# Hybrid decoder trunk on one core: the 16-block inverse multiplied from the left, and T transposed once

## What is computed

```python
    def step(state, inp):
        r_t, w_t, k_t, v_t, kk_t, b_t = inp
        sa = jnp.einsum('bhvk,bhk->bhv', state, kk_t)
        state = (state * w_t[:, :, None, :] - sa[..., None] * b_t[:, :, None, :]
                 + v_t[..., None] * k_t[:, :, None, :])
        return state, jnp.einsum('bhvk,bhk->bhv', state, r_t)
```

## Time and profile before

| | |
|---|---|
| three runs: median, lowest, highest | 1014.09, 1011.42, 1014.51 us |
| the profiled execution: its time | 1012.7 us |
| its span, from the first to the last instruction | 1010.9 us |
| TensorE busy | 973.7 us, 96% of the span |
| mean granted clock of TensorE, as a share of 2.4 GHz | 0.981 |
| VectorE, ScalarE, GpSimd busy | 262.8, 173.8, 74.5 us |
| rounds of the inverse in layer 0, in layer 1 (from the span's start) | 117.4 to 156.6, 537.5 to 576.3 us |

### The profile page before, as it was taken

One profiled execution on the slowest core, in us unless ns is written; L12 is line 12 of the kernel. 1 busy time (PEld: TensorE's weight loads), 2 busy tenths in 40 slices (PEclk: granted clock), 3 DMA queues, 4 the chain that ended last, 5 costly groups with the idle time before them and its releaser, 6 DMA issues.

```text
span 1010.9 us, 24537 instructions
## 1 busy us (share of the span) xinstructions
PE 973.7 (96%) x11036; PEld 755.0 (75%) x11036; DVE 262.8 (26%) x630; ACT 173.8 (17%) x373; POOL 74.5 (7%) x91
## 2 busy tenths in 40 slices
PE   7999999899999999999999997999999999999996
PEld 7887876488888844488877745969696977869692
DVE  2414663500000000123436635111202022120204
ACT  3354132200000000121542401000101010010101
POOL 2000610100000000000024100000000000000000
PEclk9999989999999999999998997999999999999999
DMA  9743201435544355435310028999999999999961
GB/s 319 234 126 125 84 3 43 129 118 167 166 151 138 130 206 161 136 121 155 125 57 30 3 88 326 401 401 389 412 385 401 401 400 402 400 403 385 415 242 42
DMA packets 90097, 222.79 MB, mean 220 GB/s; under 512 B 6080, under 2 KB 53952, under 8 KB 89920
## 3 DMA queue, kind: packets, MB, share of 16 engines
q1 hardware_dynamic: 84912, 211.18, 56.5%
q0 software_dynamic: 1680, 5.90, 2.4%
q10 hardware_dynamic: 3456, 4.99, 1.4%
HBM read 215.76 MB, written 6.29 MB: 220 GB/s over the span
## 4 chain that ended last, share of the span: by engine, by line
PE 94%; DVE 2%; ACT 2%; issue 1%; DMA 1%; ACTq 0%; POOL 0%; DVEq 0%; POOLq 0%; SPq 0%
PE bank L542 92%; PE bank L553 1%; PE bank L1120 1%; DMA x_sb<-in_x 1%; ACT arena L1406 0%; DVE tok L1631 0%; ACT arena L1268 0%; ACT hT L1263 0%; PE bank L902 0%; ACT arena L1403 0%; PE bank L870 0%; DVE x_sb L1605 0%; DVE arena L1831 0%; POOL small L1494 0%; ACTq L1241 0%
## 5 line engine op out<-in xcount | busy, mean ns | idle before, releaser
L542 PE MATMUL bank<-arena 128*64 128x96 f32 (+6 forms) x8804 | 523.0, 277 | 5.2 <-issue 2.3
L542 PEld LDWEIGHTS bank<-arena 128*64 128x64 f32 (+4 forms) x8804 | 393.9, 138 | 133.9 <-issue 111.5
L542 PE MATMUL bank<-hT,arena 128*128 128x256 f32 (+1 forms) x1196 | 256.1, 381 | 1.1 <-ACT hT L1263 1.1
L542 PEld LDWEIGHTS bank<-hT,arena 128*128 128x128 f32 (+1 forms) x1196 | 221.3, 188 | 34.6 <-issue 4.2
L542 PE MATMUL bank<-arena,hT 128*128 128x256 f32 (+3 forms) x556 | 136.8, 407 | 5.1 <-DVE arena L1831 3.7
L542 PEld LDWEIGHTS bank<-arena,hT 128*128 128x128 f32 (+2 forms) x556 | 89.1, 182 | 42.0 <-issue 26.5
L1605 DVE TENSOR_TENSOR arena<-arena,bank 128x256 f32<-128x256 f32 (+3 forms) x66 | 35.4, 538 | 267.2 <-ACT arena L1438 143.6
L1268 ACT COPY arena<-bank 128x512 f32<-128x512 f32 (+2 forms) x58 | 29.0, 504 | 139.3 <-PE bank L542 131.9
L1494 POOL TENSOR_TENSOR small<-small 128x1 f32<-128x1 f32 (+1 forms) x18 | 18.7, 1038 | 404.3 <-DVE small L1622 300.0
L1464 ACT ACTIVATE arena<-bank 128x480 f32<-128x480 f32 x16 | 9.1, 571 | 203.5 <-PE bank L542 203.5
L1605 DVE TENSOR_TENSOR arena<-arena 128x512 f32<-128x512 f32 (+2 forms) x50 | 32.7, 676 | 26.4 <-ACT arena L1268 25.8
(11 more groups left out here) (190 smaller groups left out, 404.3 us busy)
## 6 DMA issues: line engine op xcount, KB each, us to landing
arena<-in_moe_w SPq DMA_DIRECT2D x128, 704.0 KB, 18.0
arena<-in_moe_w SPq DMA_DIRECT2D x40, 1024.0 KB, 17.1
arena<-in_ffn_w SPq DMA_DIRECT2D x33, 1024.0 KB, 5.4
arena<-in_w_in SPq DMA_DIRECT2D x22, 1024.0 KB, 5.6
arena<-in_w_out SPq DMA_DIRECT2D x8, 1024.0 KB, 4.9
arena<-in_moe_w SPq DMA_DIRECT2D x8, 512.0 KB, 18.6
arena<-in_w_in SPq DMA_DIRECT2D x2, 1088.0 KB, 5.5
rows<-in_rows ACTq DMA_DIRECT2D x2, 642.0 KB, 6.1
```

Of the source, the lines that this page charges most:

```text
L542: return nc.tensor.matmul(o, lhsT, rhs, start=start, stop=stop, skip_group_check=True)
```

## The change

Rounds 1 to 3 now multiply T from the left and no longer keep its transpose: `T2`, `T3` and `T4` have one pair each, and the power's transpose (`N2t`, `N4t`, `N8t`) is the stationary operand. `N8` is computed transposed. VectorE adds 128 x 256 to `T` in place of 128 x 512 to `both_t`. In round 4, behind `Xa`, a new product `Tr` of T with the identity gives Tt, and ScalarE copies it to SBUF. From round 5 on both forms are kept as before. GpSimd's first sum, 1 + N, is made for T alone. The banks of the rounds from 4 on are renumbered, since `Tr` needs one.

```diff
--- before.py
+++ after.py
@@ -214,8 +214,9 @@
 MIDDLE = {2: ("KV2", 1), 4: ("S11", 1), 7: ("PT2", 0)}
 
 
-ROUNDS = (("N2",), ("N4", "T2"), ("N8", "T3"), ("T4",), ("Xa",), ("Ta",), ("Xb",), ("Tb",), ("Xc",), ("Tc",))
-ROUND_BANK = {"N2": 0, "N4": 1, "T2": 2, "N8": 0, "T3": 1, "T4": 2, "Xa": 0, "Ta": 1, "Xb": 2, "Tb": 0, "Xc": 1, "Tc": 2}
+ROUNDS = (("N2",), ("N4", "T2"), ("N8", "T3"), ("T4",), ("Xa", "Tr"), ("Ta",), ("Xb",), ("Tb",), ("Xc",), ("Tc",))
+ROUND_BANK = {"N2": 0, "N4": 1, "T2": 2, "N8": 0, "T3": 1, "T4": 2, "Xa": 0, "Tr": 1, "Ta": 2, "Xb": 0, "Tb": 1,
+              "Xc": 2, "Tc": 0}
 
 
 def build(nc, t_in, out):
@@ -288,7 +289,7 @@
 
         def inverse_buffers(base):
             v = [base[:, 256 * i:256 * i + 256] for i in range(10)]
-            return {"N": v[0], "Nt": v[1], "N2": v[2], "N2t": v[3], "N4": v[0], "N4t": v[1], "N8": v[2],
+            return {"N": v[0], "Nt": v[1], "N2": v[2], "N2t": v[3], "N4": v[0], "N4t": v[1], "N8t": v[2],
                     "T": v[4], "Tt": v[5], "E32": v[6], "E64": v[7], "X": v[8], "Bt": v[9],
                     "both_n": base[:, 0:512], "both_n2": base[:, 512:1024], "both_t": base[:, 1024:1536]}
 
@@ -821,8 +822,7 @@
 
 
             PRODUCTS = {"N2": (("Nt", "N"), ("N", "Nt")), "N4": (("N2t", "N2"), ("N2", "N2t")),
-                        "T2": (("Tt", "N2"), ("N2", "Tt")), "N8": (("N4t", "N4"),),
-                        "T3": (("Tt", "N4"), ("N4", "Tt")), "T4": (("Tt", "N8"), ("N8", "Tt")),
+                        "T2": (("N2t", "T"),), "N8": (("N4", "N4t"),), "T3": (("N4t", "T"),), "T4": (("N8t", "T"),),
                         "Xa": (("E32", "T"),), "Ta": (("Tt", "X"), ("X", "Tt")),
                         "Xb": (("E64", "T"),), "Tb": (("Tt", "X"), ("X", "Tt"))}
 
@@ -845,6 +845,12 @@
                             s = slice(h * HALF, (h + 1) * HALF)
                             last = mm(o[HALF:P, s], lg[0:HALF, c, h, HALF:P], buf["T"][0:HALF, s], start=(h == 0),
                                       stop=True)
+                    elif name == "Tr":
+                        for h in range(4):
+                            s = slice(h * HALF, (h + 1) * HALF)
+                            for q in range(0, P, HALF):
+                                r = slice(q, q + HALF)
+                                last = mm(o[r, s], buf["T"][r, s], ident[r, r], start=(h == 0), stop=True)
                     elif name == "Tc":
                         for h in range(4):
                             s = slice(h * HALF, (h + 1) * HALF)
@@ -1382,8 +1388,10 @@
                                     sem(f"block_copied{c}"), 1)
                             elif name in ("Xa", "Xb"):
                                 evacuate(f"{name}_{c}", l, buf["X"], bank(f"{name}_{c}", l)[:, 0:256])
+                            elif name == "Tr":
+                                evacuate(f"{name}_{c}", l, buf["Tt"], bank(f"{name}_{c}", l)[:, 0:256])
                             elif name == "N8":
-                                evacuate(f"{name}_{c}", l, buf["N8"], bank(f"{name}_{c}", l)[:, 0:256])
+                                evacuate(f"{name}_{c}", l, buf["N8t"], bank(f"{name}_{c}", l)[:, 0:256])
                             elif name in ("N2", "N4"):
                                 evacuate(f"{name}_{c}", l, buf["both_n2" if name == "N2" else "both_n"],
                                          bank(f"{name}_{c}", l)[:, :])
@@ -1540,8 +1548,8 @@
                 for c in range(NT):
                     buf = inv[c]
                     pool.wait_ge(sem(f"n_ready{c}"), l + 1)
-                    g.tensor_tensor(buf["both_t"].rearrange("p (h n) -> p h n", h=8),
-                                    buf["both_n"].rearrange("p (h n) -> p h n", h=8), over(const("diag_one"), 8),
+                    g.tensor_tensor(buf["T"].rearrange("p (h n) -> p h n", h=4),
+                                    buf["N"].rearrange("p (h n) -> p h n", h=4), over(const("diag_one"), 4),
                                     ALU.add).then_inc(sem(f"t_ready{c}"), 1)
                     pool.wait_ge(sem(f"t_ready{c}"), l + 1)
                     link(g.memset(first_block[c], 0.0))
@@ -1801,10 +1809,14 @@
                                 wait_full(dve, f"{name}_{c}", l)
                                 frees(v.tensor_scalar(inv[c]["Bt"][0:HALF, :], bank(f"{name}_{c}", l)[0:HALF, 0:256], -1.0,
                                                       None, ALU.mult), f"{name}_{c}", l)
-                            elif name[0] == "T":
+                            elif name in ("T2", "T3", "T4"):
+                                dst = inv[c]["T"]
+                                wait_full(dve, f"{name}_{c}", l)
+                                frees(tt(dst, dst, bank(f"{name}_{c}", l)[:, 0:256], ALU.add), f"{name}_{c}", l)
+                            elif name in ("Ta", "Tb"):
                                 dst = inv[c]["both_t"]
                                 wait_full(dve, f"{name}_{c}", l)
-                                frees(tt(dst, dst, bank(f"{name}_{c}", l)[:, :], ALU.add if r < 4 else ALU.subtract),
+                                frees(tt(dst, dst, bank(f"{name}_{c}", l)[:, :], ALU.subtract),
                                       f"{name}_{c}", l)
                         if c == 0 and r in middle:
                             middle[r](l, 2)
```

## The result

| | before | after |
|---|---|---|
| median of 7 runs each | 1012.93 us | 1002.57 us |
| lowest and highest | 1010.2, 1014.51 | 999.5, 1009.09 |
| ratio, with its 95% interval | | 0.9919 (0.9897 to 0.9941) |
| span of the profiled execution | 1010.9 us | 1000.8 us |
| mean granted clock of it | 0.981 | 0.989 |

What follows compares the result with a forecast made beforehand. TensorE, busy 96% of the span, was taken to bound the kernel. Per layer 1.23 + 1.17 + 0.97 - 0.97 - 0.1 = 2.3 us, 4.6 for both, gave 1009.5 us from the median 1014.1; range 1005.8 to 1012.5.

Steps and rivals of the forecast that it cites:

- T2 (1.23 us a layer): Round 1: T2's evacuation begins 0.97 us sooner and VectorE's narrower sum saves 0.26, so b_masks and KV1 come 1.23 sooner.
- the 1.6 us left of the wait: Ahead of KV1, TensorE would still wait for VectorE's b_masks, about 1.6 us where it waited 1.9.
- T3 (1.17): Round 2: 16 products fewer a layer, 0.49 us for tile 0 and 0.68 for tile 1, together 1.17.
- The slow share: T3 of tile 1 in the 1.2 GHz stretch: saving 0.49 to 0.88 us, taken as 0.68; tile 0 mostly at full clock.
- T4, Tr and KT's copies (0.97 - 0.97 - 0.1): Later rounds, per layer: halved T4 saves 0.97 us, added Tr costs 0.97 unhidden, ScalarE's KT copies lose 0.1.
- The sum of the work: Both layers' mixer rounds: all priced parts together save 2.3 us a layer, 4.6 us in all.
- The step that failed: Rounds after the wait before KV1: the 1.2 GHz stretch stays 6.83 us in each layer, though that wait is 0.3 us shorter.
- rival 2: Clock doesn't fall in one or both layers' rounds; 3.0 us back per layer, 1006.5 or 1003.5 us; chance 0.14.
- the signs of being wrong: Rounds: TensorE waits for VectorE before T4, b_masks begins no sooner, or time at 0.50 clock differs from 6.83 us a layer.
- the prediction's own price: Rounds at 1.2 GHz: 6.83 us hold 3.8 us of work, so a fall avoided returns 3.0 us a layer.
- The rule of the Trainium skill: PSUM evacuation: packing small tiles speeds TensorE but not the copy out, which may become the bottleneck; at its hardest, 1013.8 us.
- the third rival: T3 and T4: VectorE's evacuations replace the products, 2.14 us given back, 0.2 a layer left, 1013.8 us; chance 0.13.

Runs made afterwards that it cites:

- the kernel before with the hole filled: Kernel before plus four unread products of 128x256 ahead of KV0, keeping TensorE at work while it waits for KV1's bank: 1006.4 us (ratio 0.9934).
- T3 twice: Changed kernel with T3's products issued twice and 46 in place of 14 small warm-up products at the start: 1005.2 us (ratio 0.9915).
- the two filled kernels: Unread 128x256 products put ahead of KV0: four in the kernel before, 1006.4 us; three in the changed kernel, 1001.7 us.

## Why the prediction was wrong, point by point

- **T2 (1.23 us a layer): right in layer 1, a little low in layer 0.** KV1 stands 6.63 us behind KDT in both layers of the changed kernel. In the kernel before with the hole filled it was 8.08 and 7.84 us: 1.45 and 1.21 less. What the 0.2 us more in layer 0 are is not known. The release through VectorE, its narrow sum and the 1.6 us left of the wait came as forecast.
- **T3 (1.17): nearly twice too high.** From KV1 to QT it is 4.35 us at the full clock before and 3.74 after, 0.6 us and not 0.97. I had followed QT's operands, and left out its bank: bank 1 is KV2's until VectorE has done its sums. That wait (0.27 us) hides most of the rest. T3 twice took it back at the same price, 10.98 against 10.35 us. So this is a term mis-sized, by 0.4 us at the full clock, and the slow share of it had no place in a sum for the work. The slow share was misread too: I took tile 0's T3 as mostly at the full clock, but the clock fell at 129.11, and the loads of this tile, N8's 16 first and then T3's 32, run from 128.23 to 130.17. So most of T3 stood in the slow stretch.
- **T4, Tr and KT's copies (0.97 - 0.97 - 0.1): right as a sum.** 13.42 us before and 13.48 after at the full clock, and the wait for the exponentials is still 0.6 us. Doubling Tr confirmed that both conditions move with it. T4 and the copies were not measured by themselves.
- **The sum of the work: somewhat high.** 2.0 and 1.8 us a layer by the stages of the two filled kernels, 3.8 us in all for a forecast of 4.6. T3's error and T2's partly cancel. That the times of these kernels differ by 4.7 us is luck.
- **The step that failed** is the one by which the clock's falls stay as they are: "1.6 us are left, and there are fewer products on both sides of it", which gave rival 2 a chance of 0.14. It is what happened, in part: no fall in layer 0 and one of 3.41 us in layer 1, where there were two of 6.83. Two of the signs of being wrong that the prediction names came true: the time at 0.50 differs from 6.83 us a layer, and TensorE waits for VectorE before T4, by 0.27 us ahead of QT. Between the two profiles the four stages shrank by 8.9 us. 3.8 of it are work, and 3.0 and 1.5, by the prediction's own price, the fall that is gone and the one that is halved; the third fall is most of the 1.35 us. Over the runs the granted share rose from 0.980 to 0.987. That is 40 to 27 us at 1.2 GHz in 1010 us, 13 us less, and 13 x (1 - 1/1.8) = 6 us: the missing half. At like clock the two kernels differ by my sum or less: the one run after at 0.981 took 1009.1 us, the 13 of the kernel before in the table that had 0.981 took 1010.7 to 1013.8.
- **The range was too narrow** for another reason too: the changed kernel's runs spread over 9.6 us, and a range for it has to hold a kernel that falls and one that does not.
- **The rule of the Trainium skill** (TensorEngine Tiling, Performance Considerations), that the copy out of PSUM may become the bottleneck, had a grain: VectorE's chain is now the way from `b_masks` to QT. It cost 0.4 us a layer, not the 2.14 of the third rival. TensorE waits there for the bank that KV2 and QT share, and not for an evacuation of T2, T3 or T4. But VectorE works without a break from 123.61 us to the last sum of KV2, T3's evacuation among it, so its speed has a part in this wait.

## What to carry to other kernels

A wait that stands just ahead of a fall of the granted clock costs more than its length: here the fall's 3 us a layer were worth more than the 1.9 us of the wait, and more than the 1.9 us a layer that the removed products were. So forecast it as two cases with nearly equal chances as soon as the change shortens the wait, and try to fill or close it first. When work is taken from an engine, follow the next step's bank as well as its operands.

## What had not been expected of the hardware

- In the means over runs, a wait of 1.6 us in place of 1.9 went with a mean granted share of 0.987 in place of 0.980, and one of 2.4 us with 0.981 again; unread work put into the wait made the kernel before 8 us faster.
- The same wait was followed by a fall in one execution and not in another: 1.42 and 0.77 us ahead of 197.4 us before, with a fall of 3.41 us, and 1.43 and 0.77 after, with none.
- A float32 product of 128x256 with both operands of 128 rows took 0.43 us, in two matmuls, which the rows count apart.
- The place of a long loop in TensorE's instruction stream is worth 53 to 67 us here. 32 small products more at the start made the changed kernel 60 us slower, and the kernel before, which has 64 more than the changed one, doesn't have this delay. With it the loop's instructions are fetched anew in every pass (9 packets in the pass shown), without it only in the first.
